# Recurrence chunks of a transformer stack on one Trainium2 core: the backward direction's products moved to the other two quarters of the matrix array

## The chip, the cores and the metric

The kernel runs on one core of one Trainium2 chip. The metric is the device time of one execution, in microseconds (us). The core has a matrix engine (TensorE, PE in the views, with its weight loads as PEld), three engines for elementwise work (VectorE or DVE, ScalarE or ACT, GpSimd or POOL) and a queue engine (SyncE, SP) that starts transfers. A product on PE reads both operands from SBUF and leaves its result in PSUM; DVE and ACT take it out from there. GpSimd works on SBUF.

## The reference, cut to what matters

The whole program is a stack of two model blocks (attention, a two-way recurrence, feed-forward parts, a gated linear attention and a state-space scan). The change touches only the recurrence of the second layer. In the reference it is a scan over tokens, once forward and once backward, with a 64x64 state for each of 8 heads:

```
def step(S, inp):
    w_t, k_t, v_t, kk_t, a_t = inp[:5]
    sa = jnp.einsum('bhvk,bhk->bhv', S, kk_t)
    S = (S * w_t[:, :, None, :] - sa[..., None] * (kk_t * a_t)[:, :, None, :]
         + v_t[..., None] * k_t[:, :, None, :])
    return S, (jnp.einsum('bhvk,bhk->bhv', S, inp[5]) if emit else None)
...
s_fwd, yc_fwd = wkv7_scan(zero, cx, 0, False, need_ctx)
s_bwd, yc_bwd = wkv7_scan(zero, cx, 1, True, need_ctx)
_, y_fwd = wkv7_scan(s_fwd, lat, 0, False, True)
_, y_bwd = wkv7_scan(s_bwd, lat, 1, True, True)
```

There are 256 context tokens, of which only the final state is used, and 512 latent tokens, which also give outputs.

## The kernel before, in words

`rwkv_chunks` works in 12 chunks of 64 tokens: 4 of context, then 8 of latents. In each chunk both directions (d = 0 forward, d = 1 backward) are done side by side; they depend on each other nowhere. A tile is 128 partitions by 4 by 64: two heads lie one above the other (partitions 0 to 63 and 64 to 127, the two `corners`), four such pairs side by side. Every product is 64x64 by 64x64 (or by 64x128, called wide here). `each` (L1997 to L2004) issues the 8 products of one direction; in the views they are 16 matmuls and 16 weight loads, since an f32 product is shown as two. Corner 0 reads partitions 0 to 63 and writes 0 to 63, corner 1 reads and writes 64 to 127. So only the two quarters of the array on its diagonal are used. I call the 16 matmuls of one `each` a set.

The work on a chunk is a fixed program for each engine, in the order of the code, with semaphores between engines. On PE `core(i)` does, in order: `mv_p` (one set a direction); then five levels n = 0 to 4 which build an inverse by doubling; and then the tail. A level is: `lx` = lev times x, copied out by ACT; then `x_p` = z times lx and `z_p` = lx times z, which DVE adds to x and z (level 4 has no x). Between the `lx` sets and the rest of level n stands one piece of the preparation of the next chunk: `keys_with` (n = 0), `betas_with` (1), `turn_betas` (2), `turn_values` (3). On DVE the masks of that preparation (`mask_keys` after level 0, `mask_betas` after level 1) stand behind each direction's z update. From `lt`, which `mask_betas` writes, GpSimd makes five tiles `lev` a direction. The tail is: `au_p`, products that need nothing of it, `turn_inverse`, `gf_p`, sums, and the products with the state, after which DVE writes the new state; the next chunk's level 0 waits for it.

PE takes instructions in order: a wait holds up all that stands behind it. DVE and ACT do too.

Of the kernel before, what the change touches and what calls it, by code (L numbers as in the profile page):

```python
# [1871 lines left out]
def rwkv_chunks(nc, ident, masks_table, arrays, mixed, dec, ys):  # L1872
# [15 lines left out]
    with ExitStack() as ctx:  # L1888
# [17 lines left out]
                 "mv_p", "mv_c", "lx_p", "lx_c", "x_p", "x_c", "z_p", "z_c", "au_p", "au_c", "gf_p", "gf_c", "core_p", "cleared", "state_c",  # L1906
                 "y_c", "stored0", "stored1", "passed"]
        with stage(nc, *names) as (block, *sems):
# [83 lines left out]
            def _(pe):  # L1992
# [3 lines left out]

                def each(out, lhs, rhs, name, start=True, stop=True):  # L1997
                    apart()
                    for h in range(H):
                        for c in corners:  # L2000
                            mm = nc.tensor.matmul(out[c, h], lhs[c, h], rhs[c, h], start=start and (stop or h == 0),
                                                  stop=stop and (start or h == H - 1))
                    if name:
                        mm.then_inc(S[name], 1)  # L2004

                def pair(t):
                    return t[:].rearrange("p h a c -> p h (a c)")

                def keys_with(i, s, d, latent):
                    arrived(pe, i, s, latent)  # L2010
                    if latent:
                        each(pair(front[d]), ka[s][d], pair(ar[s][d]), "kar")
                    else:
                        each(front[d][:, :, 0, :], ka[s][d], ar[s][d][:, :, 0, :], "kar")

                def betas_with(i, s, d, latent):
                    wait(pe, "mp_ready", i, d)
                    if latent:
                        each(pair(front[d]), be[s][d], pair(ar[s][d]), "bar")
                    else:  # L2020
                        each(front[d][:, :, 0, :], be[s][d], ar[s][d][:, :, 0, :], "bar")

                def turn(out, src, name):

                    apart()
                    for h in range(H):
                        for c in corners:
                            tr = nc.tensor.matmul(out[c, h], src[c, h], ident[c, c], start=True, stop=True)
                    if name:
                        tr.then_inc(S[name], 1)  # L2030

                def turn_betas(i, s, d, latent):
                    wait(pe, "lt_ready", i, d)
                    if latent:
                        pe.wait_ge(S["q_ready"], 2 * i + (d + 1 - 2 * CC))
                    turn(front[d][:, :, 0, :], be[s][d], None)
                    turn(front[d][:, :, 1, :], ka[s][d], "bk_t")

                def turn_values(i, s, d, latent):
                    wait(pe, "kappa_c", i, d)  # L2040
                    turn(front[d][:, :, 0, :], ar[s][d][:, :, 0, :], None)
                    turn(front[d][:, :, 1, :], vf[s][d], "av_t")

                def turn_inverse(i, s, d):

                    wait(pe, "z1", i, d)
                    wait(pe, "v_c", i, d)
                    turn(front[d][:, :, 0, :], z[s][d], "x1_t")

                def core(i, s, latent, next_latent):  # L2050
                    ahead, s1 = has_next(i), 1 - s
                    for d in range(2):
                        wait(pe, "mp_ready", i, d)
                        wait(pe, "v_c", i, d)
                        if latent and not (type(i) is int and i <= CC):
                            pe.wait_ge(S["y_c"], 2 * i + (d - 1 - 2 * CC))
                        each(six[d], mp[s][d][:, :, 0, :], vt[s][d], "mv_p")
# [1629 lines left out]
```

## Time and profile before

| | |
|---|---|
| median of 3 runs | 4833.1 us (4823.01 to 4834.37) |
| the profiled execution's own time | 4830.95 us |
| its span, first to last instruction | 4829.2 us |
| share of it in the recurrence's chunks (from 1728.7 to 2164.9 us) | 436.2 us |
| PE's matmuls busy over the whole span | 4169.2 us |

Times in the rows are counted from the start of the span. A row of the timeline is one group of equal instructions, with its start, its length from the first start to the last end, the engine, the line, `out<-in` and the count; in square brackets the idle time ahead of it and what ended it. "issue" there is idle time for which the profile shows no wait. A busy PE is not a PE at its peak: a matmul is counted from its start to its end, and those of a pipeline overlap.

### The profile page before, as it was taken

The page shows a single profiled execution, that of the slowest core. Times are in us where ns is not written, and L with a number is a line of the kernel's source. Part 1 is how long each engine was busy: PE and PEld are TensorE (multiplying, and loading weights), DVE is VectorE, ACT ScalarE, POOL GpSimd, SP SyncE. Part 2 cuts the span into 40 slices and gives each one's busy share as a digit, 9 for nine tenths or more (in the row PEclk, how much of TensorE's full clock was granted, in tenths as well). Part 3 has the DMA queues.
Part 4 walks back from the last instruction along what each step waited for, and adds up shares of the span by engine and source line. Part 5 has one row for each costly group of instructions (what it writes and reads, how often), then busy time and mean ns, then how long its engine had stood idle before and what let it go on. Part 6 is the DMA issues. An engine that isn't in the chain of part 4 may idle for free. (4 is left out here: it accounts for less than half of the span.)

```text
span 4829.2 us, 85278 instructions
## 1 busy us (share of the span) xinstructions
PE 4169.2 (86%) x35880; PEld 3611.0 (75%) x35880; DVE 2249.1 (47%) x3566; ACT 1458.7 (30%) x2464; POOL 595.7 (12%) x749
## 2 busy tenths in 40 slices
PE   6786799999977668888998875799999995859999
PEld 5554588888964468886998765788888893548998
DVE  4454443334635644445444434443336854854444
ACT  2254321213234412113222333421123333633222
POOL 2010100001101332211000101100001102520000
PEclk8888899999988789998999887899999997869999
DMA  4446322222347831204332326322222344533332
GB/s 163 139 145 201 128 61 65 60 64 66 121 153 235 277 108 45 50 26 133 95 94 73 104 86 173 128 61 62 66 60 68 108 132 141 178 126 101 96 92 83
DMA packets 677460, 527.29 MB, mean 109 GB/s; under 512 B 124157, under 2 KB 600609, under 8 KB 677120
## 3 DMA queue, kind: packets, MB, share of 16 engines
q1 hardware_dynamic: 652800, 450.46, 31.1%
q0 software_dynamic: 24320, 71.89, 4.1%
q8 instruction: 264, 4.33, 0.4%
q14 instruction: 76, 0.62, 0.0%
HBM read 440.23 MB, written 82.01 MB: 108 GB/s over the span
## 5 line engine op out<-in xcount | busy, mean ns | idle before, releaser
L87 PE MATMUL acc<-h_hi,w_hi 128*128 128x258 f32 (+2 forms) x4416 | 1394.9, 316 | 45.0 <-DVE w_lo L478 33.0
L89 PE MATMUL acc<-h_hi,w_lo 128*128 128x258 f32 (+2 forms) x4416 | 1391.4, 315 | 0.0
L88 PE MATMUL acc<-h_lo,w_hi 128*128 128x258 f32 (+2 forms) x4416 | 1390.0, 315 | 0.0
L87 PEld LDWEIGHTS acc<-h_hi,w_hi 128*128 128x128 f32 x4416 | 833.2, 189 | 108.2 <-DVE w_lo L478 34.3
L88 PEld LDWEIGHTS acc<-h_lo,w_hi 128*128 128x128 f32 x4416 | 833.9, 189 | 57.8 <-issue 0.5
L89 PEld LDWEIGHTS acc<-h_hi,w_lo 128*128 128x128 f32 x4416 | 833.5, 189 | 56.1
L478 DVE TENSOR_TENSOR w_lo<-staged,w_hi 128x1024 fp32r<-128x1024 f32 (+1 forms) x414 | 488.4, 1219 | 137.1 <-ACT w_hi L356 134.0
L356 ACT CAST w_hi<-staged 128x1024 fp32r<-128x1024 f32 (+1 forms) x414 | 407.3, 1028 | 460.0 <-PE acc L89 363.6
L519 DVE COPY offset<-acc 128x2 f32<-128x2 f32 x276 | 43.7, 158 | 919.9 <-PE acc L89 916.8
L87 PE MATMUL acc<-hidden_hi,w_hi 128*128 128x512 f32 (+1 forms) x1200 | 420.2, 350 | 44.4 <-DVE hidden_lo L613 44.2
L88 PE MATMUL acc<-hidden_lo,w_hi 128*128 128x512 f32 (+1 forms) x1200 | 419.6, 350 | 0.0
L89 PE MATMUL acc<-hidden_hi,w_lo 128*128 128x512 f32 (+1 forms) x1200 | 418.6, 349 | 0.0
L87 PEld LDWEIGHTS acc<-hidden_hi,w_hi 128*128 128x128 f32 x1200 | 229.1, 191 | 74.8 <-issue 44.8
L89 PEld LDWEIGHTS acc<-hidden_hi,w_lo 128*128 128x128 f32 x1200 | 228.8, 191 | 29.5
L88 PEld LDWEIGHTS acc<-hidden_lo,w_hi 128*128 128x128 f32 x1200 | 229.3, 191 | 28.7
L419 ACT CAST hidden_hi<-up 128x768 f32 (+3 forms) x66 | 50.4, 763 | 486.9 <-DVE up L549 486.9
L530 DVE SCALAR_TENSOR_TENSOR xT<-acc,modTsecond,xT 128x512 f32<-128x512 f32 x104 | 66.5, 665 | 244.6 <-PE acc L89 244.6
L415 ACT ACTIVATE gate<-gate,offset 128x512 f32<-128x512 f32 (+1 forms) x132 | 81.3, 647 | 319.3 <-DVE gate L520 319.3
L1325 PEld LDWEIGHTS probsT_ps<-ident,probs 128*128 128x128 f32 x592 | 76.8, 163 | 125.6 <-DVE probs L1435 100.5
L1325 PE MATMUL probsT_ps<-ident,probs 128*128 128x128 f32 x592 | 109.9, 324 | 69.0 <-DVE probs L1435 58.1
L432 ACT ACTIVATE gate<-gate,offset 128x512 f32<-128x512 f32 x104 | 61.6, 631 | 335.8 <-DVE gate L520 335.8
L530 DVE SCALAR_TENSOR_TENSOR xT<-acc,modTfirst,xT 128x512 f32<-128x512 f32 x96 | 60.4, 658 | 214.7 <-PE acc L89 214.5
(473 smaller groups left out, 6143.6 us busy)
## 6 DMA issues: line engine op xcount, KB each, us to landing
staged<-in_w_ffn_in SPq DMA_DIRECT2D x88, 512.0 KB, 4.5
staged<-in_ffn_w_in SPq DMA_DIRECT2D x88, 512.0 KB, 4.7
wmod<-in_w_mod SPq DMA_DIRECT2D x8, 3072.0 KB, 11.2
wmod<-in_mod_w SPq DMA_DIRECT2D x8, 3072.0 KB, 13.1
wmod<-in_mod_w SPq DMA_DIRECT2D x16, 1536.0 KB, 10.4
staged<-in_ssd_w_in SPq DMA_DIRECT2D x42, 512.0 KB, 4.5
rows<-acum SPq DMA_DIRECT2D x40, 512.0 KB, 5.3
wmod<-in_w_mod SPq DMA_DIRECT2D x8, 2048.0 KB, 8.1
```

The source lines that it names most:

```text
L87: nc.tensor.matmul(out, w[0], x[0], start=start, stop=False)
L88: nc.tensor.matmul(out, w[0], x[1], start=False, stop=False)
L89: return nc.tensor.matmul(out, w[1], x[0], start=False, stop=stop)
L356: nc.scalar.copy(ws[s].hi[:, 0:p.KT, cols], staged[:, 0:p.KT, cols]).then_inc(S["w_hi"], 1)
L415: op = nc.scalar.activation(gate[s][:, t0:t0 + tn], gate[s][:, t0:t0 + tn], ACT.Silu, bias=offset[s][0][:, b:b + 1])
L419: nc.scalar.copy(hidden.hi[:, bass.ds(i, 1), 0:TOK - lo], up[s][:, wide]).then_inc(S["hidden_hi"], 1)
L432: op = nc.scalar.activation(into, gate[j][:, t0:t0 + tn], ACT.Identity, bias=offset[s][j][:, b:b + 1])
L478: nc.vector.tensor_tensor(ws[s].lo[:, 0:p.KT, cols], staged[:, 0:p.KT, cols], ws[s].hi[:, 0:p.KT, cols].bitcast(F32), ALU.subtract).then_i ...
L519: nc.vector.tensor_copy(offset[s][j][:], a[:, 254:256])
L530: op = nc.vector.scalar_tensor_tensor(out=xt, in0=acc[2 * s + j][:, c0:c0 + tn], scalar=p.gates[:, bass.ds(2 * i + j, 1), b], in1=xt, op0= ...
L1325: tr = nc.tensor.transpose(probsT_ps[:, k * P:(k + 1) * P], probs[n % 2][:, k * P:(k + 1) * P], ident[:])
```

## The change

The forward direction keeps its place. In the backward direction some products write to the opposite corner (`turned`): they read partitions 0 to 63 and write 64 to 127, and the other way round, which takes the two quarters off the diagonal. For this the backward direction's x, lx, values, alphas and so on lie in swapped corners where needed. `both` issues the two directions alternately, two forward and two backward, behind the later of the two waits; it replaces two calls of `each` nearly everywhere. In the levels the first product `lx` stays apart for each direction, behind its own wait, forward first (`one_of`). The forward x and z products stay as they were; the backward x (off the diagonal) and z (on it) are issued alternately. The lower triangle of the backward direction is wanted in both corners' order, so `betas_with` makes it a second time, into `big[1]`. On DVE the two masks stand behind both z updates of the level. In the tail the two products with the state stay apart, in another order (one, one, six, six), and two new semaphores (`sums_p`, `reads_p`) stand ahead of them.

```diff
+                def product(out, lhs, rhs, h, c, turned, start, stop):
+                    return nc.tensor.matmul(out[corners[1 - c if turned else c], h], lhs[corners[c], h], rhs[corners[c], h],
+                                            start=start and (stop or h == 0), stop=stop and (start or h == H - 1))
...
+                def both(out, lhs, rhs, name, start=True, stop=True):
+                    apart()
+                    for h in range(H):
+                        for d in range(2):
+                            for c in range(2):
+                                mm = product(out[d], lhs[d], rhs[d], h, c, d == 1, start, stop)
+                            if name and h == H - 1:
+                                mm.then_inc(S[name], 1)
...
-                def betas_with(i, s, d, latent):
-                    wait(pe, "mp_ready", i, d)
+                def betas_with(i, s, latent):
+                    wait(pe, "mp_ready", i, 1)
...
+                    each(big[1][:, :, 0, :], be[s][1], ar[s][1][:, :, 0, :], "bar")
+
+                def turn_betas(i, s, latent):
+                    wait(pe, "lt_ready", i, 1)
                     if latent:
+                        pe.wait_ge(S["q_ready"], 2 * i + (2 - 2 * CC))
+                    turn_both(side(front, 0), be[s], None)
+                    turn_both(side(front, 1), ka[s], "bk_t")
...
-                            each(one[d], lev[s][d][n], x[s][d], "lx_p")
+                            one_of(d, one[d], lev[s][d][n], x[s][d], "lx_p")
+                        if ahead and n < 4:
+                            (keys_with, betas_with, turn_betas, turn_values)[n](i + 1, s1, next_latent)
+                        if n == 0:
+                            wait(pe, "mv_c", i, 1)
+                        wait(pe, "lx_c", i, 0, n, LEV)
+                        if n < LEV - 1:
+                            each(six[0], z[s][0], lx[0], "x_p")
+                        each(one[0], lx[0], z[s][0], "z_p")
+                        wait(pe, "lx_c", i, 1, n, LEV)
+                        apart()
+                        for h in range(H):
+                            if n < LEV - 1:
+                                for c in range(2):
+                                    mx = product(six[1], z[s][1], lx[1], h, c, True, True, True)
+                            for c in range(2):
+                                mz = product(one[1], lx[1], z[s][1], h, c, False, True, True)
...
+                    wait(pe, "z_c", i, 1, LEV - 1, LEV)
...
+                    both(pairs(big), z[s], pairs(am[s]), "au_p")
+                    both(one, kt[s], vt[s], None, stop=False)
...
+                    wait(pe, "gf_c", i, 1)
...
+                    wait(pe, "sums_p", i, 1)
...
@@ DVE
-                            if ahead and n < 2:
+                        if ahead and n < 2:
+                            for d in range(2):
                                 (mask_keys, mask_betas)[n](i + 1, s1, d, next_latent)
```

PE in the second latent chunk, from its level 1 to the start of level 2. Tile names end in an even number for the forward direction and an odd one for the backward. Before:

```order
L2001 MATMUL one_15556<-x_15514,lev_15527 64x64 x8
L2001 MATMUL one_15557<-x_15515,lev_15532 64x64 x8
L2001 MATMUL front_15552<-ar_15464,be_15468 64x128 x8
L2001 MATMUL six_15558<-lx_15536,z_15510 64x64 x8
L2001 MATMUL one_15556<-z_15510,lx_15536 64x64 x8
L2001 MATMUL front_15553<-ar_15465,be_15469 64x128 x8
L2001 MATMUL six_15559<-lx_15537,z_15511 64x64 x8
L2001 MATMUL one_15557<-z_15511,lx_15537 64x64 x8
```

The same place of the changed kernel:

```order
L1999 MATMUL one_15556<-x_15514,lev_15527 64x64 x8
L1999 MATMUL one_15557<-x_15515,lev_15532 64x64 x8
L1999 MATMUL front_15552<-ar_15464,be_15468 64x128 x2
L1999 MATMUL front_15553<-ar_15465,be_15469 64x128 x2
...
L1999 MATMUL big_15555<-ar_15465,be_15469 64x64 x8
L1999 MATMUL six_15558<-lx_15536,z_15510 64x64 x8
L1999 MATMUL one_15556<-z_15510,lx_15536 64x64 x8
L1999 MATMUL six_15559<-lx_15537,z_15511 64x64 x2
L1999 MATMUL one_15557<-z_15511,lx_15537 64x64 x2
```

The wide products of the two directions now alternate by twos (four such pairs; two are shown), a new set into `big` follows them, the forward x and z products come behind all of that, and the backward x and z alternate.

DVE at level 1 of the same chunk, before:

```order
L2152 TENSOR_TENSOR x_15514<-x_15514,six_15558 128x256
L2156 TENSOR_TENSOR z_15510<-z_15510,one_15556 128x256
L2129 COPY lt_15504<-front_15552 128x256
L2131 TENSOR_TENSOR bq_15484<-front_15552,masks 128x4x64
L2134 TENSOR_TENSOR z_15508<-lt_15504,masks 128x256
L2136 TENSOR_TENSOR z_15508<-z_15508,masks 128x256
L2152 TENSOR_TENSOR x_15515<-x_15515,six_15559 128x256
L2156 TENSOR_TENSOR z_15511<-z_15511,one_15557 128x256
L2129 COPY lt_15505<-front_15553 128x256
L2131 TENSOR_TENSOR bq_15485<-front_15553,masks 128x4x64
```

And after:

```order
L2215 TENSOR_TENSOR z_15510<-z_15510,one_15556 128x256
L2211 TENSOR_TENSOR x_15515<-x_15515,six_15559 128x256
L2215 TENSOR_TENSOR z_15511<-z_15511,one_15557 128x256
L2187 COPY lt_15504<-front_15552 128x256
L2189 TENSOR_TENSOR bq_15484<-front_15552,masks 128x4x64
L2193 TENSOR_TENSOR z_15508<-lt_15504,masks 128x256
L2195 TENSOR_TENSOR z_15508<-z_15508,masks 128x256
L2187 COPY lt_15505<-front_15553 128x256
L2189 TENSOR_TENSOR bq_15485<-front_15553,masks 128x4x64
L2193 TENSOR_TENSOR z_15509<-big_15555,masks 128x256
```

The backward x and z updates have moved ahead of the four forward mask operations, and the backward first mask reads `big` in PSUM instead of `lt` in SBUF.

## Rows read from the trace of the kernel before

**Rows 1.** Page, its part 1: busy us, share of the span and count by engine
```profile
PE 4169.2 (86%) x35880; PEld 3611.0 (75%) x35880; DVE 2249.1 (47%) x3566; ACT 1458.7 (30%) x2464; POOL 595.7 (12%) x749
```

**Rows 2.** Windows, one to a chunk: stretch, length, busy us (count) by engine, clock
```profile
core 0: us, PE busy (x) PEld busy (x) DVE busy (x) ACT busy (x) POOL busy (x), PEclk, DMA share, GB/s
1741.20:1773.50 32.30, 28.09 (x871) 27.11 (x869) 14.86 (x34) 7.06 (x20) 8.84 (x12) 1.00 0.31 69
...
1945.90:1983.30 37.40, 33.78 (x968) 32.51 (x965) 17.66 (x38) 7.80 (x22) 9.15 (x12) 1.00 0.21 52
...
2025.10:2064.30 39.20, 35.80 (x958) 34.70 (x960) 17.10 (x37) 7.43 (x21) 7.62 (x10) 0.93 0.19 44
...
2137.20:2164.90 27.70, 24.81 (x725) 23.74 (x723) 10.91 (x26) 4.97 (x14) 1.54 (x2) 1.00 0.04 13
```

**Rows 3.** Waits of PE in the stage: total us, times, longest
```profile
PE six L2001 <- issue: 12.8, 15, 3.6
PE one L2001 <- DVE z L2156: 10.9, 11, 1.2
PE front L2028 <- issue: 10.0, 8, 1.7
```

**Rows 4.** Timeline of a latent chunk, levels 0 to 2
```profile
1947.13 1.13 PE L2001 MATMUL one<-x,lev 64*64 64x64 f32 x32
1948.06 1.14 PE L2001 MATMUL front<-ar,ka 64*64 64x128 f32 x16
...
1950.51 0.68 DVE L2121 TENSOR_TENSOR mp<-front,masks 128x512 f32<-128x512 f32 x1
...
1955.94 7.61 POOL L2237 TENSOR_TENSOR lev<-lt,masks 128x256 f32<-128x256 f32 x10 [7.32 <-DVE lt L2129]
1956.10 0.84 DVE L2134 TENSOR_TENSOR z<-lt,masks 128x256 f32<-128x256 f32 x1
...
1956.71 0.63 PE L2001 MATMUL one<-x,lev 64*64 64x64 f32 x15
1956.98 0.83 DVE L2136 TENSOR_TENSOR z<-z,masks 128x256 f32<-128x256 f32 x1
...
1957.73 0.41 DVE L2152 TENSOR_TENSOR x<-x,six 128x256 f32<-128x256 f32 x1
1958.06 0.41 DVE L2156 TENSOR_TENSOR z<-z,one 128x256 f32<-128x256 f32 x1
...
1958.57 0.75 PE L2001 MATMUL one<-x,lev 64*64 64x64 f32 x16 [1.23 <-DVE z L2156]
```

**Rows 5.** Timeline of the same chunk, level 4 and what follows it
```profile
1970.11 1.44 PE L2001 MATMUL one<-x,lev 64*64 64x64 f32 x32
...
1970.81 0.37 ACT L2216 COPY lx<-one 128x256 f32<-128x256 f32 x1 [0.75 <-PE one L2001]
1971.35 1.43 PE L2001 MATMUL one<-z,lx 64*64 64x64 f32 x32
...
1972.05 0.42 DVE L2156 TENSOR_TENSOR z<-z,one 128x256 f32<-128x256 f32 x1 [1.29 <-PE one L2001]
1972.62 1.96 PE L2001 MATMUL big<-am,z 64*64 64x128 f32 x32
```

**Rows 6.** Timeline of PE in the feature stage: column tiles of 32
```profile
1598.71 1.53 PE L1702 MATMUL mod_ps<-wmod,condsecond 128*32 128x96 f32 x64 [1.38 <-DMA wmod<-in_mod_w]
```

**Rows 7.** Timeline of PE in the gated linear attention
```profile
2940.79 0.63 PE L2550 MATMUL small<-ident,keys 64*64 64x64 f32 x16
2941.35 1.09 PE L2556 MATMUL v<-ident,vf 128*128 128x128 f32 x8
...
2943.40 2.00 PE L2577 MATMUL o<-q_scores,state_v 128*128 128x64 f32 x16
```

**Rows 8.** Timeline row behind the longest stop of PE
```profile
2025.10 1.98 PE L2001 MATMUL six<-vt,mp 64*64 64x64 f32 x32 [3.60 <-issue]
```

**Rows 9.** Windows: the stretch behind that stop
```profile
2024.00:2031.00 7.00, 5.90 (x95) 5.93 (x97) 0.00 (x0) 1.49 (x4) 0.21 (x1) 0.51 0.11 42
```

More of the change, by code:

```diff
@@ L2023, in turn @@
-                def turn(out, src, name):
+                        both(side(front, 0), ka[s], side(ar[s], 0), "kar")
+                def betas_with(i, s, latent):
+                    wait(pe, "mp_ready", i, 1)
+                    apart()
+                    wide = pairs(front), be[s], pairs(ar[s])
+                    narrow = side(front, 0), be[s], side(ar[s], 0)
+                    out, lhs, rhs = wide if latent else narrow
+                    for h in range(H):
+                        for d in range(2):
+                            for c in range(2):
+                                mm = product(out[d], lhs[d], rhs[d], h, c, d == 1, True, True)
+                            if h == H - 1 and d == 0:
+                                mm.then_inc(S["bar"], 1)
+                    each(big[1][:, :, 0, :], be[s][1], ar[s][1][:, :, 0, :], "bar")
@@ L2029, in turn @@
[L2029 to L2042, printed above, removed]
@@ L2051, in core @@
                     ahead, s1 = has_next(i), 1 - s
[L2052 to L2057, printed above, removed]
+                    wait(pe, "mp_ready", i, 1)
+                    wait(pe, "v_c", i, 1)
@@ L2058, in core @@
+                    if latent and not (type(i) is int and i <= CC):
+                        pe.wait_ge(S["y_c"], 2 * i - 2 * CC)
+                    both(six, side(mp[s], 0), vt[s], "mv_p")
                     for n in range(LEV):
@@ L2078, in core @@
-                    for d in range(2):
-                        wait(pe, "z_c", i, d, LEV - 1, LEV)
-                        each(pair(big[d]), z[s][d], pair(am[s][d]), "au_p")
-                    for d in range(2):
-                        each(one[d], kt[s][d], vt[s][d], None, stop=False)
-                        if latent:
-                            each(six[d], vt[s][d], mp[s][d][:, :, 1, :], None, stop=False)
-                    if ahead:
-                        for d in range(2):
-                            turn_inverse(i + 1, s1, d)
@@ new lines, in core @@
+                    if ahead:
+                        turn_inverse(i + 1, s1)
+                    wait(pe, "au_c", i, 1)
+                    if latent:
+                        both(pairs(big), side(au, 0), pairs(bq[s]), "gf_p")
+                    else:
+                        both(side(big, 0), side(au, 0), side(bq[s], 0), "gf_p")
+                    both(one, side(bq[s], 0), side(au, 1), "sums_p", start=False, stop=False)
+                    if latent:
+                        both(six, side(au, 1), side(bq[s], 1), "reads_p", start=False, stop=False)
@@ L2106, in _ @@
                 for part in (keys_with, betas_with, turn_betas, turn_values):
[L2107 to L2110 removed]
+                    part(0, 0, False)
+                turn_inverse(0, 0)
                 chunks(pe, core)
```

110 lines of the change are left out of this document (62 added, 48 removed).

## The prediction, as it was put on record

> **What bounds the kernel now.** I read the page first: PE is busy for 86% of the span [rows 1]. The change touches one stage, so I cut that stage into its chunks with the windows [rows 2]. The reader should see the length of a chunk beside PE's busy time: a context chunk takes 32.3 us with 28.1 of PE, a latent chunk 37.4 with 33.8 (the eight latent chunks last 36.5, 37.3, 37.4, 41.8, 39.2, 36.4, 36.5 and 27.7). DVE has 15 to 18 us in a chunk and ACT 7 to 8. So the order of PE's products sets the length, and the other engines count only where PE waits for them. The view of waits says where: 10.9 us in 11 waits for DVE's z, about one a chunk, and "issue", in which PE stands without a wait that the profile shows: five entries, 30.7 us together, 2.6 a chunk, of which the two largest are shown [rows 3]. No transfer is waited for once the stage runs.
>
> Next the pace. Two sets of `lx` start at 1947.13 and the next group at 1948.06 [rows 4]: a set takes 0.47 us of issue, so two matmuls in the two diagonal quarters take 58 ns together. A wide set takes 0.87 (1.14 less the last matmul's 0.27), 109 ns for two. A latent chunk has 52 narrow and 8 wide sets, 31.4 us. The chunk of [rows 4, 5] lasts 37.4; without its stops (breaks of 0.3 to 1.2 us inside groups of matmuls that wait for nothing, 2.5 in all) it would last 35.0.
>
> **What is taken away: issue time.** `both` puts two matmuls of each direction into four different quarters. If these run together, 32 matmuls cost the 0.47 us of one set. The trace of before has no row with all four quarters, so I bound it. Upper bound of the cost: 0.93, no overlap. Lower: 0.47. The nearest row is the column-tiled product of another stage, where four tiles of 32 columns share all rows of the array and each has its own moving operand: 64 matmuls of 96 columns in 1.53 us [rows 6]. Less the last one's 0.25 that is 20 ns a matmul, 81 for four. In the recurrence 64 moving columns take 58 ns and 128 take 109, so 96 alone would be about 84: all four ran together. Weight loads overlap there too: full-width products with 64 moving columns go at 119 ns each ((2.00 - 0.22) / 15) and with 128 at 117 [rows 7], so 128 weight columns cost about 117 ns, and four loads of 32 in series could not fit into 81. Products off the diagonal already run at a normal pace: 16 in 0.63 [rows 7]. I take 0.47.
>
> The Trainium skill, "TensorE: Matmul & The Clock Gate", Part 1, states that starts of matmuls never come closer than about 25 ns. By that, four quarters would cost 100 ns instead of 58 and nearly all of the gain would be gone. The row of the column tiles does not agree: 20 ns.
>
> With 0.47 for a pair, PE's issue in a latent chunk falls to mv 0.5, levels 11.3, keys 0.9, betas 1.3 (with the added set into `big`, 0.47), the two turns 0.9 and 1.4, au 0.9, kt, mp and inverse 1.4, gf 0.9, sums and reads 0.9, state 1.9: 22.3, which is 9 us less. Very little of this can arrive, because now the chain across the engines decides.
>
> **What the chain allows.** Handovers, from [rows 4, 5]: a set's last result is there 0.66 after its start; ACT or DVE starts 0.04 later; ACT's copy takes 0.37 and PE goes on 0.17 after it; a DVE operation takes 0.42 (0.33 apart when queued, `mp` 0.68) and PE goes on about 0.18 after it. With these I walk a latent chunk of the changed program, from level 0's first `lx`:
> - Level 0: `lx` twice to 0.94, keys to 1.81, forward x, z to 2.75; DVE's forward z ends at 3.40. Level 1 starts at 3.6 (the same walk of the old order: 4.6). The level no longer waits for PE but for DVE, by 0.3.
> - Level 1: DVE has both x and z until 4.2, then the two `mp` until 5.4. `betas_with` now needs the backward one and waits until 5.6; it and the new set end at 6.9, forward z is added at 8.5, level 2 starts at 8.7 (old order: 9.5, and the row at 1956.71 is 9.6 behind 1947.13).
> - Level 2: DVE adds backward z until 9.3, then does the forward masks. Two of these read only SBUF while GpSimd makes `lev`, and take 0.84 and 0.83 each [rows 4], until 11.6, then backward `lt` and `bq` until 12.3. `turn_betas` waits for this last one: PE stands still from 10.0 to 12.45. Before, it stood 1.2 in this level. Level 3 starts at 15.2 (old order: 15.8).
> - Level 3 has no such wait: 4.4 (before: 5.1), level 4 starts at 19.6.
> - Level 4 and tail: `au` waits for both z: 3.3 after the level's start instead of 2.5 [rows 5], 22.95. Then au, kt, mp, inverse in 2.3; `gf` waits for both `au` copies and starts at 25.6; sums and reads to 27.4; the state products wait for both `read` tiles, 28.3; from there to the next level 0 it is 3.1, as before, since y's copy and mv are on it.
> The next chunk would start at 31.4; small roundings at eight waits make it 31.7. Against 35.0 that is 3.3 us, of the 9 that PE saves. Moved DVE operations cost nothing in themselves; all the delay above is their place.
>
> The same walk for a context chunk (narrow keys, betas and gf, no `bq`, no reads) gives 27.0; before it was 32.3 to 33.2 with 3.6 of stops, 28.9 without: 1.9. Last chunk, which prepares nothing: the tail's pairs, 2.5. Start of the stage: 1.
>
> Sum: 7 x 3.3 + 4 x 1.9 + 2.5 + 1 = 34 us.
>
> **What may be given back.** Stops without a wait (2.5 us in a latent chunk, 3.6 in a context one, 3.60 at the longest [rows 3, 8]) I leave as they are. The granted clock is at its full level, 2.4 GHz, in all chunks but the one that starts at 2025.1, where it is 0.93 [rows 2]: after PE had stood for 3.60 us, 7 us ran at 0.51, that is nearly all at 1.2 GHz [rows 9]. That chunk took 39.2 where others take 36.4 to 37.4, so one fall costs about 2 to 3 us. Idle times of 1.2 to 1.7 did not bring it. The new idle of 2.4 in level 2 lies between; I take two falls in eight, 6 us. Bounds: 0 and 24.
>
> Result: 34 - 6 = 28 us less. The profiled execution took 4830.95 us (span 4829.2, 1.8 around it), 2 below the median of the three runs. 4833 - 28 = 4805; I say 4804.
>
> **The rivals.**
> *The quarters do not run together (slower).* Place: every `both`. For it: no row shows two tiles that share rows and two that share output partitions at once; the row of [rows 6] shares rows only. The walk with 0.93 and 1.75 for each pair: backward x and z end at 4.6, 10.8, 18.8 and 24.2, `turn_betas` still waits, to 15.0, and the tail adds 0.47 or 0.87 eight times: 39.3 for a latent chunk, 4.3 more than before, and 2.6 more for a context one. 7 x 4.3 + 4 x 2.6 = 41: 4874. It decides against the change once a group of four takes more than about 84 ns (58 + 58 x 34 / 75), halfway. The Trainium skill, "TensorE: Matmul & The Clock Gate", Part 3, says that a weight load overlaps running matmuls only in another row group, and this would come out of it. The sets of before do load weights for the same rows under running matmuls (58 ns for a pair of loads and matmuls with 64 columns each), and so does [rows 6], so I give it 12%.
>
> *The gain is eaten.* The pairs run, but PE asks for its instructions at twice the rate and the stops double (12 x 2.5 = 30), or the clock falls in every latent chunk (24 instead of 6). Time: 4820 to 4835. For it: the stops are there at the present pace and end nowhere in a wait. Against it: on average the chunk issues the same instructions in little less time. 20%.
>
> *The stops hide.* PE now stands in waits of 0.3 to 2.4 us several times a chunk; if the stops fall into these, up to 30 of the 37 us of stops go as well as the 34. A third to a full hiding gives 4770 to 4790. 18%.
>
> *My walk holds*, 4790 to 4818: 50%.
>
> **Numbers.** A measurement of this kernel tells about 0.3% (14.5 us) from no change. Faster by more than that: 50 + 18 and a little of the second rival, 0.70. Slower by more: the first rival, 0.12. Within: 0.18. The range 4772 to 4832 leaves out the first rival and the far end of the third.
>
> **What would show it.** Right: `six<-vt,mp` of both directions, 32 matmuls, within 0.7 us from first start to last end instead of 1.13; latent chunks of 33 to 35 us; PE's wait ahead of the `front<-ident,be` products grows from 1.2 to about 2.4 and is for DVE's `bq`; starts of levels at 3.6, 8.7, 15.2 and 19.6. Wrong: a group of four that takes more than 84 ns, stops on PE of over 3 us a chunk, or a granted clock under 0.95 in most chunks.

## The result, and the profile after

The changed kernel took 4847.38 us (median of 8 runs, 4839.99 to 4863.44), the kernel before beside it 4832.54 (8 runs). The ratio is 1.0040, with a 95% interval of 1.0024 to 1.0057: 0.4% slower. The forecast of 4804 and its range were wrong, and so was its sign. The profiled execution took 4843.77 us, with a span of 4842.0. Of the 12.8 us by which the span grew, 18.2 lie in the stage (454.6 us against 436.4, from the first `front<-ar,ka` to the last `state,grow`), 2.5 ahead of it, and the part behind it, in which nothing was changed, was 7.9 shorter.

Page of the changed kernel, its part 1, to [rows 1]:

```profile
PE 4118.6 (85%) x36072; PEld 3549.6 (73%) x36072; DVE 2234.9 (46%) x3566; ACT 1454.5 (30%) x2464; POOL 590.4 (12%) x749
```

PE lost 51 us of busy time, and the kernel got longer. Windows of the changed kernel by chunk (columns as in [rows 2]): the first context chunk, latent chunks 1, 2, 3 and 4, the last one, and then the whole stage from the first chunk on:

```profile
1746.60:1778.60 32.00, 24.95 (x888) 23.05 (x883) 14.43 (x35) 6.77 (x20) 7.50 (x10) 0.88 0.30 67
...
1878.30:1914.70 36.40, 26.25 (x987) 23.83 (x983) 17.26 (x40) 7.38 (x22) 7.42 (x10) 1.00 0.21 47
1914.70:1955.20 40.50, 30.17 (x980) 28.49 (x981) 16.42 (x38) 7.32 (x22) 8.98 (x12) 0.83 0.20 49
1955.20:1994.30 39.10, 27.25 (x976) 25.13 (x976) 16.05 (x38) 7.44 (x22) 8.96 (x12) 0.96 0.21 51
1994.30:2039.20 44.90, 31.89 (x976) 30.13 (x976) 16.69 (x39) 7.61 (x22) 10.51 (x14) 0.81 0.20 50
...
2156.30:2185.90 29.60, 22.04 (x712) 20.25 (x714) 9.89 (x24) 4.18 (x12) 1.54 (x2) 0.88 0.03 12
...
1746.50:2186.00 439.50, 323.99 (x11083) 301.43 (x11078) 184.68 (x430) 83.25 (x246) 92.69 (x124) 0.89 0.17 41
```

The clock column is the first thing to see. It was at 1.00 in all chunks of before but two (0.99 and 0.93); now only one chunk has 1.00, and it is the shortest latent chunk of full length. The waits of PE in the stage, to [rows 3]:

```profile
PE six L1999 <- issue: 33.5, 23, 3.6
PE one L1999 <- issue: 24.4, 20, 3.4
PE front L2035 <- DVE bq L2189: 18.3, 8, 2.3
PE big L1999 <- DVE z L2215: 7.3, 12, 0.6
PE one L1999 <- DVE z L2215: 4.5, 12, 0.4
PE front L2035 <- DVE lt L2187: 4.1, 3, 1.4
```

Summed over all rows of this view, idle time without a wait ("issue") went from 30.4 us to 63.0, and waits for other engines from 11.6 to 47.2. That closes the account: PE's busy time fell by 52.8 (376.8 to 324.0), idle without a wait rose by 32.6 and waits by 35.6, and 15.4 us is what the stretch of the chunks grew (424.1 to 439.5).

The timeline of PE in latent chunk 3, to [rows 4]:

```profile
1955.17 0.71 PE L1999 MATMUL six<-vt,mp 64*64 64x64 f32 x32 [0.55 <-ACT y L2285]
...
1960.09 0.21 PE L1999 MATMUL six<-lx,z 64*64 64x64 f32 x1 [1.46 <-issue]
...
1960.49 0.63 PE L1999 MATMUL one<-x,lev 64*64 64x64 f32 x16
...
1962.81 1.99 PE L1999 MATMUL front<-ar,be 64*64 64x128 f32 x32 [0.56 <-DVE mp L2179]
...
1967.40 1.39 PE L1999 MATMUL one<-x,lev 64*64 64x64 f32 x32
1971.11 0.69 PE L2035 MATMUL front<-ident,be 64*64 64x64 f32 x32 [2.31 <-DVE bq L2189]
1971.60 0.67 PE L2035 MATMUL front<-ident,ka 64*64 64x64 f32 x32
```

The first and the last two rows show the pairing at work: 32 matmuls in 0.71, 0.69 and 0.67 us. The stop at 1960.09 falls inside a group that waits for nothing. What happens to the clock behind it shows in three windows of equal length:

```profile
1958.90:1962.30 3.40, 1.72 (x54) 1.47 (x53) 1.66 (x5) 0.39 (x2) 0.00 (x0) 1.00 0.01 1
1962.30:1965.70 3.40, 2.89 (x54) 2.92 (x56) 0.37 (x1) 0.36 (x1) 0.00 (x0) 0.50 0.02 5
1965.70:1969.10 3.40, 2.97 (x96) 2.60 (x92) 2.64 (x7) 0.64 (x2) 0.67 (x1) 1.00 0.02 5
```

In the first PE is busy for half of the time, in the second it runs at 0.50 of its clock (1.2 GHz), and the third is at full clock again. The group of `front<-ar,be` that begins in the second takes 1.99 us; the same group took 1.10 in latent chunk 1, which ran at full clock. The DMA view of the stretch just ahead of that stop, 1957.40 to 1958.90, has this row of queue 8:

```profile
q8 instruction: 1, 0.02, 5.9%
```

One packet of 16 KB of instructions, which in the trace starts at 1957.45 and ends at 1958.87; PE goes on 1.22 us behind its end. The stage has 91 such packets (90 before). 51 idle times of PE of more than 0.3 us, 65.9 us in all, end between 1.05 and 1.7 us behind the end of such a packet; before, 30 did, with 26.8 us. I call these the tied stops. Eight of the 51 (7.5 us) are waits for another engine that end there. The other 43 are nearly all that PE stands without a wait: of its 44 such stops of more than 0.3 us, 43 are tied, where ends spread evenly would put about one in seven into that stretch (0.65 of 4.8 us from packet to packet). The Trainium skill, "Vector Engine (DVE) Microarchitecture Reference", section "Instruction fetch and dispatch (NX sequencer)", gives an instruction, there one of VectorE, 64 bytes. The trace of PE agrees with that size: 11,083 matmuls and 11,078 weight loads at 64 bytes make 87 packets of 16 KB, and 91 are there, which also hold PE's other instructions.

### The profile page after: what moved, and what is told of

It reads as the page before. It is cut to its first block and busy times, and to the rows that moved or that the text cites. A ratio compares the mean times of both kernels' runs of the same rounds, so it can differ in the third digit from the quotient of the medians.

```text
span 4842.0 us, 85448 instructions
## 1 busy us (share of the span) xinstructions
PE 4118.6 (85%) x36072; PEld 3549.6 (73%) x36072; DVE 2234.9 (46%) x3566; ACT 1454.5 (30%) x2464; POOL 590.4 (12%) x749
## 5 line engine op out<-in xcount | busy, mean ns | idle before, releaser
L1325 PEld LDWEIGHTS probsT_ps<-ident,probs 128*128 128x128 f32 x592 | 75.6, 161 | 126.4 <-DVE probs L1435 102.9
## 6 DMA issues: line engine op xcount, KB each, us to landing
wmod<-in_w_mod SPq DMA_DIRECT2D x8, 3072.0 KB, 11.6
```

The lines of the kernel that those rows point to most:

```text
L1325: tr = nc.tensor.transpose(probsT_ps[:, k * P:(k + 1) * P], probs[n % 2][:, k * P:(k + 1) * P], ident[:])
```

## Experiments

"Stage" is measured as above; the columns behind it are for the stretch of the chunks. "Falls" counts, in the trace's clock records of that stretch, how often the clock went to 1.2 GHz, and beside it stands all the time spent there (for after, e1, s1, s3 and t1 some 4 us of it belong to a low stretch that began ahead of the first chunk). Ratios are to the kernel before on the same chip. All columns but the ratio are of one profiled execution of each kernel, and the executions of one kernel differ: the changed kernel's eight times spread over 23 us.

| kernel | ratio (95%) | stage us | idle without a wait | waits | falls, us at half clock | tied stops, us |
|---|---|---|---|---|---|---|
| before | | 436.4 | 30.4 | 11.6 | 1, 6.8 | 30, 26.8 |
| after | 1.0040 (1.0024-1.0057) | 454.6 | 63.0 | 47.2 | 18, 92.8 | 51, 65.9 |
| e1 | 1.0028 (1.0013-1.0043) | 441.9 | 47.6 | 40.4 | 9, 41.7 | 44, 43.9 |
| e2 | 0.9999 (0.9983-1.0014) | 437.8 | 72.1 | 32.9 | 13, 51.2 | 57, 68.7 |
| e3 | 0.9990 (0.9975-1.0005) | 440.2 | 66.8 | 27.4 | 6, 20.5 | 59, 65.1 |
| e4 | 0.9983 (0.9971-0.9995) | 430.3 | 60.2 | 47.2 | 7, 37.5 | 60, 62.3 |
| e6 | 0.9963 (0.9949-0.9978) | 420.8 | 59.5 | 31.5 | 3, 10.2 | 56, 60.8 |
| e7 | 0.9948 (0.9931-0.9965) | 425.7 | 51.4 | 47.3 | 10, 51.2 | 51, 57.0 |
| e8 | 1.0060 (1.0037-1.0083) | 458.1 | 71 | 15 | 14, 55.1 | 52, 67.5 |
| e9 | 1.0017 (1.0002-1.0033) | 446.4 | 51.1 | 12.3 | 7, 27.3 | 33, 48.3 |
| e10 | 0.9855 (0.9825-0.9886) | 366.2 | 11.9 | 50.2 | 8, 34.1 | 8, 10.9 |
| e11 | 0.9981 (0.9970-0.9992) | 424.4 | 56.4 | 33.2 | 5, 20.5 | 54, 59.0 |
| e12 | 1.0008 (0.9995-1.0021) | 433.0 | 27.9 | 12.0 | 3, 10.2 | 27, 30.8 |
| s1 | 1.0054 (1.0037-1.0070) | 449.4 | 60.9 | 47.5 | 17, 85.9 | 55, 60.1 |
| s2 | 1.0057 (1.0037-1.0078) | 451.9 | 43.3 | 11.3 | 2, 10.2 | 44, 42.9 |
| s3 | 1.0031 (1.0014-1.0049) | 443.4 | 59.8 | 44.8 | 15, 69.3 | 58, 58.9 |
| s4 | 1.0079 (1.0050-1.0107) | 457.7 | 57.3 | 13.5 | 10, 41.0 | 30, 53.5 |
| t1 | 0.9874 (0.9849-0.9898) | 362.6 | 7.6 | 49.8 | 8, 35.0 | 5, 4.4 |
| t2 | 1.0023 (1.0010-1.0037) | 439.7 | 75.6 | 23.3 | 10, 37.5 | 60, 71.1 |

**e1, the same waits without alternation.** In every joint group the backward products follow the forward ones:

```diff
-                    for h in range(H):
-                        for d in range(2):
+                    for d in range(2):
+                        for h in range(H):
                             for c in range(2):
```

> The changed kernel, but in each joint group the backward products come behind the forward ones and not in turn with them; every wait and every place in the order stays. Theory A (PE is short of instructions when four quarters run at once, and each stop and wait then also costs clock): the idle without a wait in the stage falls from 64 us to about 31 as in the kernel before, the granted clock of the stage rises from 0.88 to 0.96 or more; the groups cost 0.93 instead of 0.47, by my walk 41 us more over the stage, so the time is between 0 and 10 us above the changed kernel's 4847. Theory B (the longer joint waits alone are what costs): stops stay near 64, the clock under 0.92, and the time rises by 30 us or more.

The stage is 5.5 us longer than before's and 12.7 shorter than after's. The joint waits and the moved operations alone bring nine falls. Tied stops are at 43.9 us here, but the unchanged program reaches 42.9 by being moved (s2, below), so how the growth of the stops divides between the waits and the alternation is not shown. Even unalternated, a group of 32 can pass in about 1 us (`six<-vt,mp` from 1950.59 to 1951.57; before it took 1.13 or more), so the pairing's worth on PE is smaller than full serial groups would suggest.

**e2, DVE takes `lt` and `bq` of both directions ahead of the other masks.**

```diff
+                    if d == 0:
+                        take_lower(i, s, 0, latent)
+                        take_lower(i, s, 1, latent)
                     wait(dve, "lt_ready", i, d)
```

> The changed kernel, but DVE takes lt and bq of both directions before the four mask operations on z, so that turn_betas on PE can start earlier. Both theories: the wait ahead of the turns of be falls from 2.3 us to about 0.6 in a latent chunk. Theory B (joint waits cost): 8 x 1.7 + 4 x 1 = 18 us less and fewer falls of the clock, 4825 us. Theory A (instruction supply sets the pace): the stops take part of the room, stops grow from 64 to 70 us or more, and the time falls by 5 to 10 us.

Its waits for `bq`, to the 18.3 us of after, and its two largest rows:

```profile
PE six L1999 <- issue: 35.6, 27, 4.0
PE one L1999 <- issue: 27.1, 21, 3.0
...
PE front L2035 <- DVE bq L2189: 5.3, 8, 0.7
```

13 us of the wait are gone, the stage is 16.8 us shorter than after's, and the ratio is 1.000. The idle time without a wait grew, from 63.0 us to 72.1. So the changed kernel comes back to the time of before by the place of the `lt` and `bq` operations alone, with 13 falls left.

**e3, PE kept busy through the wait.** Four full-width products whose results nobody reads, ahead of `turn_betas`' wait:

```diff
                 def turn_betas(i, s, latent):
+                    for _ in range(4):
+                        nc.tensor.matmul(big[0][:, :, 0, :], ident[:], ka[s][0][:], start=True, stop=True)
                     wait(pe, "lt_ready", i, 1)
```

> The changed kernel with four full-width products of 256 columns (8 matmuls, about 1.7 us) in front of PE's wait for the turns of be; their result is not used. They fill the longest wait with work and need few instructions. If the falls of the clock come from this wait: fewer than 8 falls instead of 16 or so in the stage, clock over 0.94, 10 us less. If they come from the stops, which this does not touch: at least 10 falls stay, clock about 0.90, and the time moves by less than 5 us.

Its stage in one window:

```profile
1741.20:2167.10 425.90, 325.52 (x11173) 293.16 (x11166) 184.11 (x430) 83.05 (x246) 92.70 (x124) 0.98 0.18 42
```

The clock is back at 0.98, and the stage 14.4 us shorter than after's, with the idle time without a wait as long as before this edit (66.8). The waits are 19.8 us less only because PE fills them with the added products. Each of the six falls that are left has a stop of 1.6 to 3.7 us without a wait just ahead of it. By this about 14 of the 18 us that the stage had grown are the clock's; the runs on placement below say how firm such a difference is.

**e8, more of the same**: one such product ahead of `betas_with`' wait too, and two ahead of `au`'s.

> The changed kernel with fillers (full-width products of 256 columns whose result is not used): four ahead of the turns of be, one ahead of the betas, two ahead of au. Theory C (falls of the clock follow PE's idle stretches and cost the time): falls go from 18 (6 with the first filler alone) to 3 or fewer, and the stage is 3 to 6 us shorter than the 440 of the first filler. Theory A: what is left over my walk's 405 are the stops, 65 us or more, and they do not shrink.

Waits fell to 15 us, but falls rose to 14, against the 3 or fewer expected, and the stage is 17.9 us longer than e3's. 71 us of stops are left, and covering waits does not take these away. PE's matmuls are busy for 353.5 us in the stretch of the chunks, 28.0 more than in e3, in part by the lower clock; the rest is the added products themselves.

**e4, the preparation of the next chunk by direction.** `keys_with`, `betas_with`, the two turns and DVE's masks go back to one direction at a time, as before the change, forward behind the forward level products. The levels' backward x and z, `mv` and the tail stay joint.

```diff
+                        if ahead and n < 4:
+                            (keys_with, betas_with, turn_betas, turn_values)[n](i + 1, s1, 1, next_latent)
                         wait(pe, "lx_c", i, 1, n, LEV)
```

> The changed kernel, but the preparation of the next chunk (keys, betas, two turns) and DVE's masks are again done direction by direction, each behind its own wait and in the old places; levels' backward x and z, mv and the tail stay joint. Theory A: fewer joint groups, stops about 45 us, clock 0.93, and 4830 to 4840 us. Theory B: the wait for DVE ahead of the turns is gone, about 15 us less: 4825 to 4832.

The stage came to 430.3, 6 us under before's, with 60.2 us of idle time without a wait where the theory of instruction supply had expected about 45.

**e6, joint groups in `mv` and the tail alone.** e4, and the levels' backward x and z no longer alternate:

```diff
                                     mx = product(six[1], z[s][1], lx[1], h, c, True, True, True)
+                        for h in range(H):
                             for c in range(2):
```

> The last kernel (preparation split by direction), with the backward x and z products of the levels also one behind the other; joint groups are left in mv and the tail alone. If the stops grow with the share of joint groups: stops 50 us (there 60), waits on DVE a little less, 4818 to 4824. If joint x and z bring time on the level chain: 5 us slower than the last kernel, 4824 or more.

Its stage in one window, and its largest waits:

```profile
1743.50:2152.50 409.00, 312.88 (x11086) 294.21 (x11082) 185.08 (x430) 84.91 (x246) 93.50 (x126) 0.99 0.19 44
```

```profile
PE one L1999 <- issue: 31.2, 32, 2.5
PE six L1999 <- issue: 17.4, 15, 3.4
PE one L1999 <- DVE z L2211: 16.4, 14, 1.6
PE big L1999 <- DVE z L2211: 7.3, 12, 0.6
```

33.8 us less in the stage than the changed kernel and 15.6 less than before. It has nearly all of after's idle time without a wait, but no wait for an engine of over 1.6 us, and the clock stays at 0.99.

**e5, the opposite: the kernel before with a semaphore increment behind every product.** It was to slow the stream of PE's matmuls.

```diff
                             mm = nc.tensor.matmul(out[c, h], lhs[c, h], rhs[c, h], start=start and (stop or h == 0),
                                                   stop=stop and (start or h == H - 1))
+                            pe.sem_inc(S["passed"], 1)
```

> The kernel before, with one more instruction on PE behind every product of the stage: an increment of a semaphore that nobody waits for. The matrix work, the waits and the order are the same; PE's instruction stream is a quarter longer. Theory A (stops without a wait come from the supply of instructions): stops rise from 30 us to 50 or more, the stage from 436 to 450 or more, time 4840 to 4850. If the supply doesn't matter: stops within 5 us of 30 and the time within 0.1% of before, unless an increment itself slows the pace of a set, which the length of a set (0.47 us) shows.

The increments cost far more than expected. A timeline row of a wide set (0.87 us of issue before) and the window of the stage:

```profile
2000.55 1.46 PE L2001 MATMUL front<-ar,be 64*64 64x128 f32 x16
```

```profile
1750.10:2729.70 979.60, 968.64 (x10902) 924.23 (x10901) 199.76 (x430) 87.67 (x247) 95.07 (x124) 0.60 0.08 19
```

The stage took 1000.1 us. Idle time without a wait all but vanished (6 us), so in a slow enough stream the stops do not show (111 packets in 979.6 us, one for every 8.8); but with a clock of 0.60 and a ratio of 1.116 the kernel says nothing of stops at the old pace.

**e9 and e10, half the instructions.** The kernel before and the changed one with one matmul for two heads, at twice the columns. This leaves out the products with the weights of every second pair of heads, so the result is not the recurrence's; e9, e10, s4 and t1 show times only:

```diff
-                    for h in range(H):
+                    for h in range(0, H, 2):
                         for c in corners:
-                            mm = nc.tensor.matmul(out[c, h], lhs[c, h], rhs[c, h], start=start and (stop or h == 0),
+                            mm = nc.tensor.matmul(out[c, h:h + 2], lhs[c, h], rhs[c, h:h + 2], start=start and (stop or h == 0),
```

> The kernel before with half of PE's instructions in the stage and the same moving columns: each product takes two neighbouring head pairs' columns against the weights of the first, so every set has 8 matmuls of twice the width and lasts about 0.44 us as before (left out: the products with the weights of every second head pair; turns write zeros there). Waits, order and the other engines are unchanged. Theory A (stops without a wait are the supply of instructions): stops fall from 30 us to 10 or less, the stage from 436 to about 412, the time to about 4808. If stops have another cause they stay near 30 and the time within 0.1% of before.

> The changed kernel with the same halving of instructions (again only the weights of every second head pair are used). Theory A: stops from 63 us to 20 or less, the clock over 0.95, and the stage where my walk had it less the stops: 400 us or less, time near 4795. If the stops are something else: 60 us stay and the time is 4840 or more. The difference to the halved kernel of before is then what the pairing and its waits bring when instructions are not short: my walk says 30 us less.

The largest waits of e9:

```profile
PE one L2001 <- issue: 16.7, 13, 2.2
PE six L2001 <- issue: 14.6, 9, 3.2
PE one L2001 <- DVE z L2156: 11.3, 11, 1.3
```

and of e10:

```profile
PE front L2035 <- DVE bq L2189: 18.5, 8, 2.3
PE big L1999 <- DVE z L2215: 7.5, 12, 0.8
PE six L1999 <- issue: 7.2, 4, 3.4
```

In the order of before, half the instructions and half the packets (46) brought more idle time without a wait, 51.1 against 30.4: the number of instructions in a microsecond, my rival's mechanism, does not by itself say how long PE stops. In the changed order it nearly vanished, 11.9, and the stage took 366.2. In e10 the walk across the engines is what is left: it has after's waits (50.2) and after's `bq` wait. Between the two halved kernels the change takes 80.2 us off the stage, where 30 were expected; 39.2 of these are stops, and the other 41 are near the 34 of the walk. In these kernels, where the pairing does not bring more stops, its gain arrives.

**e7, e11, e12, the chunk loop written out**, for e4, e6 and the kernel before. PE's stream then has no jump and no registers in its waits.

```diff
-                with eng.Fori(CC // 2 + 1, NCH // 2 - 1) as t:
-                    for s in range(2):
-                        body(2 * t + s, s, True, True)
-                for i in range(NCH - 2, NCH):
+                for i in range(CC + 2, NCH):
                     body(i, i % 2, True, True)
```

> The kernel with the preparation split by direction, with the two passes of the chunk loop written out, on all engines. If the longest stop (3.4 to 4.0 us, at the loop's way back) and the fall of the clock behind it come from the loop: no stop over 3 us in the stage, 3 to 7 us less, 4812 to 4816. If written-out code costs as much supply: within 2 us of 4819.

> The kernel with joint groups in mv and the tail alone (preparation and levels by direction), with the chunk loop written out. If both gains add: 0.37% and 0.35%, together 0.7% under before, 4795 to 4800. If written-out code only shifts stops: 4812 or more.

> The kernel before with the chunk loop written out. If the stop at the loop's way back (3.6 us) and the fall of the clock behind it (2 to 3 us) go away: 6 us less than before, 4820 to 4824 where before is 4829. If written-out code costs as much: the same time as before within 0.1%.

The kernel before is the same without its loop (27.9 us of idle without a wait), so the loop is not the cause of the stops. e7 has the lowest ratio of all that do the whole work, 0.9948, but e11, which should have been better by e6's lead on e4, has 0.9981. In the profiled executions e11's stage is the shorter one, 424.4 against 425.7, so the difference is not the stage's. Its cause is open; the next runs show how much can move with nothing changed in the work.

**s1 to s4, nothing changed but where instructions lie.** 128 (s3: 64) increments on PE ahead of the stage: s1 and s3 of the changed kernel, s2 of the kernel before, s4 of e9.

```diff
+                for _ in range(128):
+                    apart()
                 for part in (keys_with, betas_with, turn_betas, turn_values):
```

> The changed kernel with 128 increments on PE ahead of the stage, where PE waits over 20 us for its first transfer anyway. They only move the program by half a 16 KB block of instructions against the blocks' borders. If the stops (each ends 1.1 to 1.7 us behind the end of a 16 KB instruction packet) depend on where the borders fall by chance: idle without a wait moves by 10 us or more from 63, and the time by 5 or more from 4847, either way. If they come from the faster pace and the joint waits, wherever the borders are: 60 to 66 us, and the time within 3 us.

> The same 128 increments ahead of the stage in the kernel before. Chance of the borders: idle without a wait well away from 30 us (45 or more) and the time 5 us or more above before. Otherwise 28 to 33 us and the time of before within 0.1%.

> The changed kernel moved by 64 increments, a quarter of a block. Chance of the borders: another value again, 10 us or more from both neighbours. Otherwise 60 to 66 us of idle without a wait.

> The kernel before with half of PE's instructions in the stage (only the weights of every second head pair are used) and 128 increments ahead. Without the shift it had 51 us of idle without a wait, 33 of its 46 blocks of instructions with a stop, against 12 us in the changed kernel halved the same way. If this is chance of the borders: under 30 us here. If it belongs to the kernel's form: 45 to 55.

The waits and the stage of s2, the kernel before moved by 128 instructions:

```profile
PE one L2001 <- issue: 19.3, 21, 2.3
PE six L2001 <- issue: 14.2, 11, 4.2
PE one L2001 <- DVE z L2158: 10.7, 11, 1.2
```

```profile
1754.00:2194.80 440.80, 381.19 (x10915) 365.91 (x10913) 197.71 (x430) 87.68 (x247) 94.67 (x124) 0.99 0.17 41
```

The increments themselves take up to 14 us ahead of the stage (it starts at 1742.8 in s2, 1728.8 before), so "placement" here is two things that these runs do not part: where instructions lie, and a later start (in s3 the start moved by 0.6 us only). Inside it the same program stops for 43.3 us instead of 30.4, and the stage takes 451.9 instead of 436.4. The changed kernel went the other way, 454.6 to 449.4 and (s3) 443.4. At the same shift of 128 the two kernels take the same time, 4851.9 and 4850.0. So a difference of 10 to 15 us between two stages, as in e1 to e4, can be placement's. What does not move with it: the changed kernel has 60 to 63 us of idle without a wait in three placements and 15 to 18 falls; the kernel before, here and written out, 28 to 43 us and 1 to 3 falls.

**t1 and t2, e10 and e6 moved by 128.**

> The changed kernel with half of TensorE's instructions at the same columns (the weights of every second pair of heads are left out of the products, as in e10_half_after), and 128 semaphore increments ahead of the stage, so that every instruction of it lies elsewhere in the stream. If e10's 11.9 us of idle time without a wait come from the number of instructions, as 48 packets of instructions in place of 91, the idle time stays under 20 us and the stage near 370 us. If they come from where the instructions happen to lie, as in the halved kernel before (51.1 us, and 57.3 shifted), the idle time comes out at 30 us or more and the stage at 385 us or more. The median is 4755 us plus up to 14 us for the increments in the first case.

> e6_tail_only (joint groups for the product by the values and the tail alone) with 128 semaphore increments ahead of the stage. The kernel before took 451.9 us for the stage with the same 128 increments and 436.4 without; e6 took 420.8 without. If e6 gains by its form, its stage stays at least 8 us under 451.9 and its median under the 4850 us of the kernel before with the same increments. If its gain was one of placement, the stage comes out within 8 us of 451.9 or over it.

The largest waits of t1:

```profile
PE front L2035 <- DVE bq L2191: 18.5, 8, 2.3
PE big L1999 <- DVE z L2217: 7.2, 12, 0.6
...
PE six L1999 <- issue: 5.1, 2, 3.7
```

e10's lack of stops is no luck of placement: 7.6 us here. Its counterpart in the old order keeps 57.3 (s4). e6 moved is 12.2 us under s2 in the stage and 12.7 in the median (4837.4 against 4850.0, on two chips; by the ratios 0.34%), as far as it was ahead unmoved (0.37%); with the loop written out it is 0.27% (e11 against e12). The gain of e6 is of its form. Its own stage moved by 18.9 us, from 420.8 to 439.7.

## Why the prediction was wrong

**Right: how the profile was read, and the pairing.** A pair of sets takes the time of one: 32 matmuls in 0.71 us, which less the last one's 0.22 is 16 ns a matmul; the forecast was under 0.7 for the group, 0.47 of issue. The rival *The quarters do not run together* is out. The Trainium skill's floor of about 25 ns ("TensorE: Matmul & The Clock Gate", Part 1) does not hold here either: 31 starts of 25 ns would be 0.78. The prediction set its price too low: by its own formula, 58 + 58 x 34 / 75, a group of four at 100 ns would have cost more than all of the gain, not nearly all.

**Right: the walk.** Latent chunk 1 ran at full clock. Its rows, levels 1 and 2 and the wait behind:

```profile
1883.66 1.40 PE L1999 MATMUL one<-x,lev 64*64 64x64 f32 x32
1885.61 1.10 PE L1999 MATMUL front<-ar,be 64*64 64x128 f32 x32 [0.56 <-DVE mp L2179]
...
1888.66 1.39 PE L1999 MATMUL one<-x,lev 64*64 64x64 f32 x32
1892.32 0.89 PE L2035 MATMUL front<-ident,be 64*64 64x64 f32 x32 [2.26 <-DVE bq L2189]
```

From level 1 to level 2 it is 5.0 (forecast 5.1), from level 2 to `turn_betas` 3.66 (3.75), with 2.26 of wait for `bq` (2.45), and level 3 starts at 1895.16, 6.5 later than level 2 (6.5). The chunk took 36.4 with 4.8 us of idle time without a wait; without it, 31.6, where the walk said 31.7.

**Wrong: "Stops without a wait ... I leave as they are."** This is the step that failed first. They are 4.8 us in that chunk where the same chunk of before had 2.5, and 63.0 in the stage instead of 30.4. (The prediction's figures for before do not agree among themselves: it adds the view of waits to 30.7 us and later speaks of 37. For the chunk of [rows 4, 5] it has 2.5, and the view of waits has 1.9.) The prediction had the case as its second rival, *The gain is eaten*, with 30 us for a doubling; 32.6 came. It had weighed it at 20% on the argument that "on average the chunk issues the same instructions in little less time". Stops, though, are not set by the average: e9 issues half the instructions and stops longer than the kernel before. Placement has a part in the size: moved by 128 instructions, the two kernels have 43.3 us and 60.9.

**Wrong: "I take two falls in eight, 6 us."** There were 18 falls with 92.8 us at 1.2 GHz, and six of the twelve chunks at 0.81 to 0.88. The rival's two halves were offered as alternatives (doubled stops, or falls), and both happened; most of the falls stand behind stops. The price per fall was sized well enough, as 82 us more at half clock behind the falls can cost 41 at most, 2.4 for each of 17 more falls, but e3 shows 14; that part of the slow time passes in waits that are there anyway would explain it, and is not shown. What brought a fall was judged from one instance, the 3.60 us of [rows 8, 9], and from "idle times of 1.2 to 1.7 did not bring it". Of the 18, six have a 2.3 us wait for `bq` just ahead of them, ten a stop of 1.5 to 3.6 us, and two no more than a stop of 0.8 and a wait of 0.6. The new idle of 2.4 us that the prediction had put between its two cases brought a fall in six of eight places; it had reckoned with two.

**The sum.** 34 us of the walk, less 32.6 for stops, less 14 for the clock, gives 13 us longer, and the stage grew by 18.2. The 5 us between are not settled, and the 14 rest on one kernel. e2 took 16.8 us off the same stage in another way, by shortening the wait, with 13 falls left. And placement alone moves a stage by up to 19 (e6 and t2). The range of 4772 to 4832 failed for that too: it had no term for where instructions lie.

**How much of the 0.4% is the change's.** More stops and many more falls show in both placements in which the two kernels can be compared: 63.0 us against 30.4 and 18 falls against 1, and, both moved by 128 instructions, 60.9 against 43.3 and 17 against 2. The sign of the total does not: moved, the two take the same time. Shown is that the pairing's gain on PE does not arrive; that it costs 0.4% holds for this placement.

**What stays open.** Why PE waits for some packets and not for others. Not the loop (e12), not the number of instructions alone (e9, s4), not placement alone (s1, s3, t1), and not the packet's own length: in after, packets with a tied stop took 1.11 us on average and those without one 1.11 as well. Order and number together change it (e10 and t1 against e9 and s4), and a slow stream hides it (e5).

## What to carry to other kernels

Idle time of PE without a wait is a term of the sum: take it per chunk from the view of waits, and price a change that shortens PE's stream with these stops growing up to the whole gain, as they did here (32.6 of 34 us). Before joining the two directions' groups behind the later wait, ask for each group whether both inputs are there at that time: where they nearly are (`mv` and the tail here, with a wait of 0.6 us for z) the kernel with pairing was 0.3 to 0.4% faster than before (e6, t2), though no run tells the pairing's part in this from that of e6's other edits. Where they are not, it makes a 2.3 us wait, and PE's clock fell behind six of eight such. A difference of some tenths of a per cent in a kernel of this sort is to be measured at two or three placements, since 128 instructions ahead of a stage made that stage of the unchanged program 15.5 us longer, 0.3% of the whole, on top of up to 14 us that they took themselves.

## What the runs showed of the hardware

- Four 64 x 64 f32 quarters of the array, all in use at once, rows and columns both shared, take a matmul every 16 ns (0.71 us for 32).
- Instructions reach PE in packets of 16 KB, about 1 us each, one for some 4.8 us of the stage (91 in 439.5; 46 in e9, with half the instructions). 51 of the 91 were followed by an idle time of PE that ended 1.05 to 1.7 us behind the packet, 43 of them without a wait. 128 instructions more ahead changed the number: 44 of 91 in the kernel before, where it had been 30 of 90.
- Increments between matmuls are dear: a narrow set went from 0.47 us to about 1.4 with 8 increments in it, one behind each product; part of this is the clock. It was at 0.60 there, though the records have PE busy for 968.64 of 979.60 us: a busy PE in the records does not keep the clock up.
- A single wait of 2.3 us was enough for the clock to fall to 1.2 GHz behind it, and twice a wait of 0.6 with a stop of 0.8 was; but two of the eight waits of 2.3 us brought no fall. A fall lasted 4.9 us on average (18 falls, 88.7 us).
